# Head attentions of a two-block transformer: steps of two query tiles, values streamed against turned probabilities, scaling at the end, and the turned copies shared by ScalarE and VectorE

## The reference, cut to what matters

```python
def block(q):
    p = jax.nn.softmax(gqa_scores(q, k_all), axis=-1)
    return gqa_out(p, v_all)
...
s_nb = jnp.einsum('brwhd,brwyxhd->bhrwyx', qblk, kn).astype(jnp.float32) + bias[None]
...
p = jax.nn.softmax(jnp.concatenate([s_loc, s_ctx, sink_q], -1), axis=-1)
return gqa_out(p[..., :span], vb) + gqa_out(p[..., span:span + C], v_ctx)
```

## Time and profile before

| | |
|---|---|
| median of 3 runs | 2620.39 us (2618.93 to 2620.96) |
| the profiled execution | 2621.06 us |
| its span in the trace | 2619.3 us |
| TensorE busy | 2505.5 us, 96% |
| VectorE busy | 1626.1 us, 62% |
| ScalarE busy | 1275.3 us, 49% |
| mean granted TensorE clock | 0.988 of full |

### The profile page before, as it was taken

How to read it: one execution, slowest core, us unless ns; L and a number is a source line. 1 busy time by engine, 2 the same in 40 slices (tenths; PEclk the granted TensorE clock), 3 DMA queues, 4 the chain that set the end, 5 groups by cost and what they waited for, 6 DMA issues and landing times.

```text
span 2619.3 us, 41629 instructions
## 1 busy us (share of the span) xinstructions
PE 2505.5 (96%) x15930; PEld 2079.9 (79%) x15930; DVE 1626.1 (62%) x2680; ACT 1275.3 (49%) x2372; POOL 253.6 (10%) x266
## 2 busy tenths in 40 slices
PE   6999999999989999999999999899999999999998
PEld 4855678889957999889886687688889899778887
DVE  2657565553688786768776863533326799775664
ACT  3356454433657765533336743422225644675554
POOL 3000100001302100315000001000002330011000
PEclk8999999999999999999999999999999999999999
DMA  7265522224555555534324534522236555634555
GB/s 282 89 227 185 193 96 96 96 88 133 159 178 194 168 180 170 174 109 150 121 97 143 159 122 171 207 96 96 92 94 172 165 178 172 204 107 143 184 173 149
DMA packets 137895, 393.58 MB, mean 150 GB/s; under 512 B 13776, under 2 KB 40400, under 8 KB 137616
## 3 DMA queue, kind: packets, MB, share of 16 engines
q1 hardware_dynamic: 135872, 386.47, 45.5%
q0 software_dynamic: 1872, 5.02, 0.7%
HBM read 390.39 MB, written 1.05 MB: 149 GB/s over the span
## 4 chain that ended last, share of the span: by engine, by line
PE 82%; DVE 8%; ACT 4%; DMA 3%; issue 2%; POOL 1%; SPq 0%; ACTq 0%; DVEq 0%; POOLq 0%
PE bank L647 21%; PE bank L649 20%; PE bank L648 20%; PE bank L644 4%; PE bank L695 3%; PE bank L854 2%; DVE w_low L1863 2%; PE bank L643 2%; PE bank L864 2%; PE bank L879 1%; ACT w_high L1163 1%; DVE smax L2130 1%; PE bank L877 1%; DMA ring<-in_w_down 1%; PE bank L835 1%
## 5 line engine op out<-in xcount | busy, mean ns | idle before, releaser
L1863 DVE TENSOR_TENSOR w_low<-ring,w_high 128x1024 fp32r<-128x1024 f32 (+2 forms) x604 | 688.1, 1141 | 523.8 <-ACT w_high L1163 520.7
L647 PE MATMUL bank<-h_high,w_high 128*128 128x512 f32 (+1 forms) x2576 | 884.2, 343 | 36.2 <-DVE h_low L2060 8.1
L649 PE MATMUL bank<-h_high,w_low 128*128 128x512 f32 (+1 forms) x2576 | 870.5, 338 | 0.0
L648 PE MATMUL bank<-h_low,w_high 128*128 128x256 f32 (+1 forms) x2432 | 821.6, 338 | 0.0
L1163 ACT CAST w_high<-ring 128x1024 fp32r<-128x1024 f32 (+2 forms) x604 | 574.5, 954 | 302.2 <-DMA ring<-in_w_down 146.8
L647 PEld LDWEIGHTS bank<-h_high,w_high 128*128 128x128 f32 x2576 | 493.8, 192 | 98.3 <-issue 24.9
L649 PEld LDWEIGHTS bank<-h_high,w_low 128*128 128x128 f32 x2576 | 493.8, 192 | 50.4
L648 PEld LDWEIGHTS bank<-h_low,w_high 128*128 128x128 f32 x2432 | 465.6, 191 | 49.4 <-issue 1.7
L647 PE MATMUL bank<-f_high,w_high 128*128 128x256 f32 (+1 forms) x616 | 194.7, 316 | 4.1 <-DVE w_low L1863 3.5
L649 PE MATMUL bank<-f_high,w_low 128*128 128x256 f32 (+1 forms) x616 | 193.0, 313 | 0.0
L648 PE MATMUL bank<-f_low,w_high 128*128 128x256 f32 (+1 forms) x528 | 168.1, 318 | 0.0
(11 more groups left out here) (285 smaller groups left out, 3495.4 us busy)
## 6 DMA issues: line engine op xcount, KB each, us to landing
ring<-in_w_up SPq DMA_DIRECT2D x176, 512.0 KB, 3.4
ring<-in_w_mod SPq DMA_DIRECT2D x112, 512.0 KB, 4.2
ring<-in_w_down SPq DMA_DIRECT2D x80, 384.0 KB, 3.1
ring<-in_w_down SPq DMA_DIRECT2D x80, 320.0 KB, 3.0
spare_slabs<-in_w_mod SPq DMA_DIRECT2D x48, 512.0 KB, 8.0
ring<-in_w_gate SPq DMA_DIRECT2D x48, 512.0 KB, 3.4
ring<-in_w_k SPq DMA_DIRECT2D x32, 512.0 KB, 3.5
ring<-in_w_v SPq DMA_DIRECT2D x32, 512.0 KB, 3.4
```

Source lines behind the costliest of these rows:

```text
L647: pe.matmul(out, wh[:, cols], high, start=first, stop=False)
L648: pe.matmul(out, wh[:, cols], low, start=False, stop=False)
L649: ins = pe.matmul(out, wl[:, cols], high, start=False, stop=last)
L1863: v.tensor_tensor(wl[:, cols], raw[:, cols], wh[:, cols].bitcast(F32), ALU.subtract).then_inc(low_ready, 1)
```

## The change

The units of the head attentions become steps of a pair of heads and two tiles (`head_steps`): 16 in layer 0, in turn with 512 and 256 keys, and 8 in layer 1, with 512 keys. A set of four score and probability buffers holds one "use": one tile of both heads with 512 keys, or both tiles side by side with 256. So a step with 512 keys has two uses, one with 256 keys has one.

The scaling of the probabilities goes. The value product now loads the turned probabilities (128 keys by 128 queries) and streams the values (64 features), so that queries lie on the partitions of the output; there VectorE scales by the inverse sums, four times 64 columns a step (`store`). Two more transposes a step turn the output back (`output_turn`), ScalarE copies its high half straight from PSUM (`high`), VectorE makes the low half from PSUM (`low`). Of the turned probabilities, ScalarE copies the first head's (bank 5) and VectorE the second's (bank 6). Eight probability and eight turned buffers take the place of six and four. The exponentials of the sinks are made four at once from differences. The modulation slabs are dealt out by a list (`slabs`), 3 or 4 a step, with 3 (layer 0) and 4 (layer 1) ahead of the attention, before the waits for the value copies and the rotated queries. The mixing products wait for the low halves step by step. Nothing else changes in what is computed.

```diff
         PROB = [HS[:, i, :] for i in range(6)]
         PROBT = [HS[:, 6 + i, :] for i in range(2)]
-        PAIR_PROBT = PROBT + [SC[:, 2 + i, :] for i in range(2)]
-        PAIR_SCORES = [bank[i] for i in (2, 3, 4, 1)]
+        HEAD_PROB = PROB + [SC[:, i, :] for i in range(2)]
+        HEAD_PROBT = PROBT + [SC[:, 2 + i, :] for i in range(4)] + [TMP[:, i, :] for i in range(2)]
+        HEAD_SCORES = [bank[i] for i in (2, 3, 4, 1)]
...
+            def modulation_beside(A, first, last):
+
+                for k in range(first, last):
+                    if k and k % 16 == 0:
+                        pe.wait_ge(rows_copied, n["rows"] + k // 16)
+                    mod_slab(A.beside[k // 16], k % 16)
+
+            def attend_heads(name):
+
+                A = PAIRED[name]
+                e0, p0 = n["sub"], n["unit"]
+
...
+                def output_turn(j):
+                    pe.wait_ge(o_ready, p0 + j + 1)
+                    for x in range(2):
+                        ins = pe.transpose(OUTB[:, S + x * P:S + x * P + P], TOKEN_OUT[j % 2][:, x * P:x * P + P], IDENT)
+                    ins.then_inc(o_turned, 1)
+
...
+                def turn(j):
+                    for s, _ in A.of(j):
+                        for i in range(2):
+                            k = 2 * s + i
+                            pe.wait_ge(ex_ready, e0 + k + 1)
+                            if s:
+                                pe.wait_ge((pt_ready, pt_vector)[i], n["copied"] * (1 - i) + n["vector_copied"] * i + s)
+                            for t in range(TT):
+                                ins = pe.transpose(bank[5 + k % 2][:, t * P:(t + 1) * P], HEAD_PROB[k % 8][:, t * P:(t + 1) * P], IDENT)
+                            ins.then_inc(tr_done, 1)
+
+                def values(j):
+                    uses, last = A.of(j), A.steps[j]["T"] // P - 1
+                    pe.wait_ge(pt_ready, n["copied"] + uses[-1][0] + 1)
+                    pe.wait_ge(pt_vector, n["vector_copied"] + uses[-1][0] + 1)
+                    if j:
+                        pe.wait_ge(o_halved, n["halved"] + j)
+                    for s, tiles in uses:
+                        for x in tiles:
+                            for i in range(2):
+                                at = (2 * x + i) * HD
+                                for t in range(last + 1):
+                                    b = tiles.index(x) * (last + 1) + t
+                                    ins = pe.matmul(OUTB[:, at:at + HD], HEAD_PROBT[(2 * s + i) % 8][:, b * P:(b + 1) * P],
+                                                    A.steps[j]["v"][i][t], start=(t == 0), stop=(t == last))
+                    ins.then_inc(pv_done, 1)
+
...
+                scores(0)
+                for j in range(A.count):
+                    if j + 1 < A.count:
+                        scores(j + 1)
+                    modulation_beside(A, A.slabs[j + 1], A.slabs[j + 2])
+                    if j >= 2:
+                        output_turn(j - 2)
+                    turn(j)
+                    if j:
+                        values(j - 1)
+                output_turn(A.count - 2)
+                values(A.count - 1)
+                output_turn(A.count - 1)
...
                     values_by_token("ev_v", VALUES1)
+                    modulation_beside(PAIRED["block1"], 0, PAIRED["block1"].slabs[1])
                     pe.wait_ge(value_copied, n["value"])
                     pe.wait_ge(rope_done, n["rope"])
...
+                def copy(j):
+                    for s, _ in A.of(j):
+                        act.wait_ge(tr_done, t0 + 2 * s + 1)
+                        if s >= 4:
+                            act.wait_ge(pv_done, p0 + A.owner[s - 4] + 1)
+                        nc.scalar.copy(HEAD_PROBT[2 * s % 8], bank[5][:, :]).then_inc(pt_ready, 1)
+
+                def high(j):
+                    n["turned_out"] += 1
+                    act.wait_ge(o_turned, n["turned_out"])
+                    nc.scalar.copy(OH[:, A.steps[j]["chunk"], A.steps[j]["tokens"]], OUTB[:, S:TOK]).then_inc(o_high, 1)
...
+            def attend_heads(name, opens):
+
+                A = PAIRED[name]
+                e0, t0, p0 = n["sub"], n["turned"], n["unit"]
+
+                def copy(j):
+                    for s, _ in A.of(j):
+                        dve.wait_ge(tr_done, t0 + 2 * s + 2)
+                        if s >= 4:
+                            dve.wait_ge(pv_done, p0 + A.owner[s - 4] + 1)
+                        v.tensor_copy(HEAD_PROBT[(2 * s + 1) % 8], bank[6][:, :]).then_inc(pt_vector, 1)
+
+                def maxima(j, uses):
+                    step = A.steps[j]
+                    for s, tiles in A.of(j)[uses]:
+                        for i in range(2):
+                            sc, at = HEAD_SCORES[(2 * s + i) % 4], (4 * j + 2 * tiles[0] + i) % NS
+                            dve.wait_ge(sc_done, e0 + 2 * s + i + 1)
+                            if step["masks"] is not None:
+                                own.link(v.tensor_tensor(sc[:, 0:S], sc[:, 0:S], step["masks"][tiles[0]][i], ALU.add))
+                            if len(tiles) == 1:
+                                ins = v.reduce_max(smax[:, at:at + 1], sc[:, :], AX_X, negate=True)
+                            else:
+                                ins = v.reduce_max(smax[:, at:at + 3:2], streams(sc[:, :], 2), AX_X, negate=True)
+                            if step["sink"] is None:
+                                ins.then_inc(nm_ready, 1)
+                            else:
+                                own.inc(ins)
+                        if step["sink"] is not None:
+                            m = smax[:, at - 1:at + 1]
+                            minus = nsink[:, :].rearrange("p (i c) -> p c i", i=2)[:, step["sink"], :]
+                            own.wait(own.n)
+                            own.link(v.tensor_tensor(m, m, minus, ALU.min))
+                            v.tensor_tensor(ssink[:, at - 1:at + 1], m, minus, ALU.subtract).then_inc(nm_ready, 2)
+
...
+                def store(j):
+                    dve.wait_ge(pv_done, p0 + j + 1)
+                    own.wait(inverted[j])
+                    for a in range(4):
+                        ins = v.tensor_scalar(TOKEN_OUT[j % 2][:, a * HD:(a + 1) * HD], OUTB[:, a * HD:(a + 1) * HD],
+                                              srec[:, (4 * j + a) % NS:(4 * j + a) % NS + 1], None, ALU.mult)
+                    ins.then_inc(o_ready, 1)
+
+                def low(j):
+                    n["high_out"] += 1
+                    dve.wait_ge(o_high, n["high_out"])
+                    c, tokens = A.steps[j]["chunk"], A.steps[j]["tokens"]
+                    v.tensor_tensor(OH[:, 8 + c, tokens], OUTB[:, S:TOK], OH[:, c, tokens].bitcast(F32),
+                                    ALU.subtract).then_inc(o_halved, 1)
+
...
+                inverted = {}
+                maxima(0, slice(0, 2))
+                for j in range(A.count):
+                    if j + 1 < A.count:
+                        maxima(j + 1, slice(0, 1))
+                    if j >= 2:
+                        low(j - 2)
+                    if j + 1 < A.count:
+                        maxima(j + 1, slice(1, 2))
+                    copy(j)
+                    inverse_sums(j)
+                    inverted[j] = own.n
+                    if j:
+                        store(j - 1)
+                    if j == A.count - 1:
+                        begin(LIN[opens], ahead, (0,))
+                low(A.count - 2)
+                store(A.count - 1)
+                begin(LIN[opens], ahead, (1,))
+                low(A.count - 1)
+                n["sub"] += 2 * A.uses
```

More of the change, by code:

```diff
@@ L472, in units_pair @@
                     keys = slice(0, TOK) if qt < 2 else slice(S, TOK)
-                    k0 = keys.start // P
+                    count, k0 = (keys.stop - keys.start) // P, keys.start // P
                     v0 = vcols + (0 if shared else c * P)
@@ L476, in units_pair @@
                     out.append(dict(
[L477 to L482, removed]
@@ L483, in units_pair @@
-                        rows=halves, out=O[:, chunk0 + c, qt * P:(qt + 1) * P]))
-            return out
+                        subs=[[(G[rows, qchunk + c, t * P:(t + 1) * P], G[rows, kchunk + (0 if shared else c), keys])
+                               for rows in halves] for t in (qt, qt + 1)],
+                        T=count * P, sink=c if sink else None,
+                        masks=None if qt >= 2 or mask is None else [[mask(2 * c + i, t) for i in range(2)] for t in (qt, qt + 1)],
+                        v=[[VT[:, k0 + t, v0 + HD * i:v0 + HD * i + HD] for t in range(count)] for i in range(2)],
@@ new lines, in head_steps, with __init__, of, copied @@
+                        chunk=chunk0 + c, tokens=slice(qt * P, (qt + 2) * P)))
+            return out
+        class Heads:
+            def __init__(self, steps, beside, shares):
```

(24 more changed lines are left out.)

197 lines of the change are left out of this document (109 added, 88 removed).

## The result

The changed kernel takes 2704.83 us (median of 3 runs, 2704.38 to 2711.24) against 2620.39: a ratio of 1.0331, with a 95% interval of 1.0307 to 1.0355. It is slower, as forecast, but by 84 us where the forecast added 55; its time lies above the range of 2652 to 2693.

What follows compares the result with a forecast made beforehand. TensorE, busy 96% of the span, was taken as the bound. Layer 1's +31.8 and layer 0's +22.9 us sum to +54.7 on 2621.1, giving 2675.8, or 2675 as the median of runs; range 2652 to 2693.

Steps and rivals of the forecast that it cites:

- Then 0.51 for the last turn and 3.69 of products: 12.73: Layer 1's step: full-price work behind TensorE's 2.40 us wait, 12.73 us a step where two units took 8.17.
- The half clock: Rival, chance 0.18: about half of 4 us behind each of six layer-1 waits lost too, 10 to 14 us; about 2687.
- the start: Layer 1's start: scores of two steps before any product, and exponentials waited for, 13.5 us.
- the six steps: Layer 1's six steps of 12.73 us, each with its wait and nothing recovered: 76.4 us.
- the end: Layer 1's end: 10.2 us of work and 5.8 of waits with nothing to cover the chain, 16 us.
- The products: Value products in both layers: 640 records at 0.1125 us instead of 0.064, 0.09 more a group; 32 us added.
- The wait: Layer 1: TensorE waits 2.40 us a step for VectorE's copy before the second head's transposes, in six steps.
- ScalarE hides: Layer 0: ScalarE has 5 us of work in a 12.7 us step, so it adds no time.
- Layer 0: Layer 0's head attention stage: 133.1 us and 0.8 for slabs moved ahead, against 111.0: +22.9 us.
- small waits: Rival, chance 0.12: VectorE reaches its copy early, leaving TensorE's own 32 + 6 us and the ends; about 2660.
- half way: Rival, chance 0.07: value products stay at the old 0.064 us a record, with the new waits; about 2640.
- priced by streaming: Rival, chance 0.05: records cost by streamed columns, halving 0.064 to 0.032; 2606 without growing waits, 2631 with VectorE's order.

Runs made afterwards that it cites:

- e7_both: The changed kernel with VectorE's first-use copy ahead of the second use's maxima and the values loaded again (output not the reference's): 2639.88 us, ratio 1.009.
- e4_values_loaded: The changed kernel with values loaded and turned probabilities streamed in its value products, as before the change (output not the reference's): 2655.3 us, ratio 1.0144.
- e2_copy_first: The changed kernel with VectorE copying the first use's turned probabilities before the second use's maxima instead of behind them: 2668.18 us, ratio 1.0196.
- e1_fill: The changed kernel with 18 more products, adding zeros, in TensorE's wait in steps 3, 4 and 5 of layer 1's attention: 2683.88 us, ratio 1.0259.

## Why the prediction was right and wrong

Four of the kernels make a square: new products or old, with the wait or without.

```text
                       no wait                  wait of 2.4 us a step
values loaded          e7_both                  e4_values_loaded
  whole kernel         2639.9 us                2655.3 us
  above its before     22.3 us                  37.7 us
  a step of layer 1    9.17 us, clock 1.00      13.0 us, clock 0.87
probabilities loaded   e2_copy_first            the change
  whole kernel         2668.2 us                2704.8 us
  above its before     49.9 us                  84.4 us
  a step of layer 1    10.03 us, clock 1.00     17.6 us, clock 0.69
```

The products cost 27.6 us, the wait 15.4; together they cost 62.2, which is 19.2 more than the two apart. Layer 1's stage alone says the same: 87.4, 99.2, 105.0 and 137.2 us, 20.4 more together than apart. The rest, 2639.9 - 2617.6 = 22.3, is the step structure; by the profiled executions, which differ by 18.2, 5.1 of it lie in layer 0 (116.1 against 111.0 us) and 11.7 in layer 1 (87.4 against 75.7).

*The step that failed* is the pricing of layer 1's step: "Then 0.51 for the last turn and 3.69 of products: 12.73". The sum was nearly right for the full clock (e1_fill: 12.45), and the work behind the wait did not get it. The rival *The half clock* named the mechanism and the place, but was given 0.18 and "10 to 14 us". It was held down by "in layer 0 waits of under 0.6 a step cost no clock", though those are not waits of 2.4, while the earlier trace rows showed a low clock behind one of 1.97. Its price took half of the 4 us behind the wait; the trace shows nearly all 3.7 us of products at the half clock (2.4 to 3.2 more) and the next scores too (1.2 to 1.8 more), in two steps also some of the slabs behind them. Laid against the forecast, layer 1 (137.2 against 105.9) divides into 17.9 - 13.5 = 4.4 at the start, 97.5 - 76.4 = 21.1 in the six steps and 21.8 - 16 = 5.8 at the end, with the end counted from the last step's close. (The first two steps take 11.3 and 16.0 us, the others 17.3 to 17.7.) The steps' 21.1 are the clock: in e1_fill, where three of them are filled, the stage takes 120.0 us instead of 137.2. The end's 5.8 are the clock too: its output turns, turns, two groups of products, statistics product and column turn take 6.1 us more from start to start than the same groups at the full clock, and one wait of 0.33 us is hidden by it, so that the 16 were right for the full clock. The start's 4.4 are waits for exponentials of 3.40, 1.56 and 1.48 us and a low clock:

```profile
771.45 1.13 PE L889 MATMUL bank<-big 64*128 64x512 f32 x4 [3.40 <-ACT h_space L1592]
774.14 2.08 PE L889 MATMUL bank<-big 64*128 64x512 f32 x4 [1.56 <-ACT h_space L1592]
```

Most of them stay in e2_copy_first too (16.8 us to the same point, also with a low clock), so that term does not come from the copy's wait and was simply mis-sized.

*The products:* forecast 32 us, measured 27.6 without the wait and 22.6 in the old structure. The price of a record was right (0.113 and 0.114 against 0.1125). A step grows by 0.86 from e7 to e2, where the sum had 1.64. Of the difference 0.26 is that the neighbours get cheaper, which the sum did not have: scores behind such products take 1.91 instead of 2.08 us, the turns next to them 1.01 instead of 1.10. Another 0.45 is no saving of the new products: in the step order the old ones cost 2.50 us (e7) and not 2.05.

*The wait:* forecast 2.40 in six steps, measured 2.41 in five and 0.80 in the first. It is no luck: in the first of the five (scores at 795.11) TensorE stands in front of those turns 6.0 us behind the start of the scores and starts them at 8.4, where the sum had 6.13 and 8.53. *ScalarE hides* and *the rest of the program is unchanged*: both held. *Layer 0:* +19.8 for +22.9, by the small scores and the same discount. *The other rivals:* small waits is refuted by the 2.41, half way and priced by streaming by the 0.114.

The Trainium skill (TensorE: Matmul & The Clock Gate, section A second HAM failure mode: psum-queue depth-cycling) says that frequent short idles between groups of matmuls can make the granted clock swing between its two levels. By that rule the trace agrees, with 0.69 to 0.77 in steps whose longest idle is 2.41 us, though an idle of 0.33 in every step left 1.00 (e2_copy_first); it would have spoken for the rival.

## What to carry to other kernels

A wait of TensorE that recurs has two prices: its length, and what the work behind it costs at the lower clock. Here they were 2.4 and 5 us a step, and the second was 1.5 with the other kind of products. When a new order puts such a wait into a stage, read in the trace of before what the granted clock did behind a wait of like length, and price all of the work behind it at both levels. A copy that another engine waits for belongs ahead of that engine's own work for the next step; and work that is only to be done some time (the slabs) belongs into the wait, which gave 28 of the 84 us back here, and not ahead of it.

## What the runs showed that was not expected

Giving TensorE 2.3 us more to do in a step made the step 5 us shorter (17.6 to 12.45). The same wait of 2.41 us left a granted clock of 0.87 with 64 loaded and 128 streamed columns and of 0.69 with 128 loaded and 64 streamed; without the wait both left 1.00. And with the values loaded, records whose heads take turns cost 0.064 us in the kernel before, those of one head after the other 0.078 in e7_both; that the order is the reason was not shown.
